# One state-space piece between the halves of the compression weights, keys and values turned two units earlier

## What is computed

```
xn = rms_norm(x, mix_norm_g)
a_q, a_kv, a_g, l_x, l_g, s_z, s_xbc, s_dt, m_g = [xn @ w for w in split(w_in)]
y_a = nsa_branch(a_q, a_kv, a_g, ...)     # attention: compressed, selected, window
y_b = rglru_branch(l_x, l_g, ...)         # causal conv, gates, recurrence
y_c = ssd_branch(s_z, s_xbc, s_dt, ...)   # causal conv of s_xbc, state-space mixer
x = x + merge(y_a, y_b, y_c, m_g) @ w_out
x = x + peer_ffn(rms_norm(x), ...)

# in nsa_branch, for keys and for values (n_cmp = 15 blocks of 32 positions):
blk = t[:, cmp_idx] + pe
compress = gelu(blk @ w1) @ w2            # w1 is 2048 x 256
k_cmp = rms_norm(compress(k_c, ...)); v_cmp = compress(v_c, ...)
```

## Time and profile before

| | us |
|---|---|
| median of three runs (2522.91 to 2526.2) | 2523.36 |
| the profiled execution | 2521.18 |
| its span | 2519.3 |

### The profile page before, as it was taken

The page is one execution under the profiler, slowest core; times in us unless marked ns, Lnnn a source line. Parts: engine busy times, 40 slices in busy tenths (PEclk is TensorE's granted clock), DMA queues, the critical chain, the costliest instruction groups (busy, mean ns, idle before and its releaser), DMA issues.

```text
span 2519.3 us, 43785 instructions
## 1 busy us (share of the span) xinstructions
PE 2464.8 (98%) x18006; PEld 2290.4 (91%) x18006; DVE 1591.2 (63%) x2554; ACT 1314.9 (52%) x1934; POOL 797.9 (32%) x436
## 2 busy tenths in 40 slices
PE   8899999999999999999998999999999999999999
PEld 8898999999999998888898989999999999888887
DVE  6878676498244555555677886764973455555555
ACT  5486663444554444444554965644445444444443
POOL 0011200288888830000000112003888888200000
PEclk9999999999999999999999999999999999999999
DMA  6533345355444445566555333453554444555554
GB/s 254 187 134 118 101 143 184 133 185 180 168 141 142 143 168 194 193 213 233 184 184 184 120 127 107 148 178 134 185 184 161 141 143 143 176 192 193 194 194 171
DMA packets 95956, 419.26 MB, mean 166 GB/s; under 512 B 10768, under 2 KB 11152, under 8 KB 78864
## 3 DMA queue, kind: packets, MB, share of 16 engines
q1 hardware_dynamic: 95760, 416.47, 48.0%
HBM read 415.38 MB, written 1.05 MB: 165 GB/s over the span
## 4 chain that ended last, share of the span: by engine, by line
PE 91%; DVE 4%; DMA 3%; ACT 2%; POOL 0%; issue 0%; SPq 0%; DVEq 0%
PE bank L2034 26%; PE bank L365 18%; PE bank L367 18%; PE bank L366 18%; PE bank L2015 5%; DMA xr<-in_xstream 1%; PE bank L761 1%; PE bank L738 1%; PE bank L722 1%; DVE ring_lo L356 1%; DMA ring<-in_wstream 1%; PE bank L1878 1%; PE bank L778 1%; PE bank L857 1%; PE bank L870 1%; POOL xr_lo L1736 0%
## 5 line engine op out<-in xcount | busy, mean ns | idle before, releaser
L1731 ACT ACTIVATE xr_hi<-xr 128x1024 fp32r<-128x1024 f32 x512 | 542.6, 1060 | 782.4 <-DMA xr<-in_xstream 782.1
L1736 POOL TENSOR_TENSOR xr_lo<-xr,xr_hi 128x1024 fp32r<-128x1024 f32 x256 | 620.7, 2428 | 428.3 <-ACT xr_hi L1731 427.8
L365 PE MATMUL bank<-featH,xr_hi 128*128 128x256 f32 x2048 | 586.7, 286 | 2.6 <-POOL xr_lo L1736 2.6
L366 PE MATMUL bank<-featL,xr_hi 128*128 128x256 f32 x2048 | 575.6, 281 | 0.0
L367 PE MATMUL bank<-featH,xr_lo 128*128 128x256 f32 x2048 | 575.5, 281 | 0.0
L1736 DVE TENSOR_TENSOR xr_lo<-xr,xr_hi 128x1024 fp32r<-128x1024 f32 x256 | 313.6, 1225 | 303.2 <-ACT xr_hi L1731 302.9
L365 PEld LDWEIGHTS bank<-featH,xr_hi 128*128 128x128 f32 x2048 | 386.2, 189 | 3.3 <-issue 1.8
L366 PEld LDWEIGHTS bank<-featL,xr_hi 128*128 128x128 f32 x2048 | 386.2, 189 | 0.0
L367 PEld LDWEIGHTS bank<-featH,xr_lo 128*128 128x128 f32 x2048 | 386.1, 189 | 0.0
L365 PE MATMUL bank<-featH,ring_hi 128*128 128x256 f32 x1232 | 354.5, 288 | 17.4 <-DVE ring_lo L356 16.2
L366 PE MATMUL bank<-featL,ring_hi 128*128 128x256 f32 x1232 | 348.8, 283 | 0.0
(11 more groups left out here) (347 smaller groups left out, 3986.0 us busy)
## 6 DMA issues: line engine op xcount, KB each, us to landing
xr<-in_xstream SPq DMA_DIRECT2D x512, 512.0 KB, 3.3
ring<-in_wstream SPq DMA_DIRECT2D x128, 1024.0 KB, 4.9
smw<-in_small SPq DMA_DIRECT2D x4, 617.0 KB, 9.1
first<-in_wstream SPq DMA_DIRECT2D x4, 512.0 KB, 7.0
first<-in_wstream SPq DMA_DIRECT2D x2, 1024.0 KB, 8.2
subk<-in_subkeys SPq DMA_DIRECT2D x2, 1024.0 KB, 7.0
x<-in_x SPq DMA_DIRECT2D x2, 512.0 KB, 6.0
big<-in_mix_row SPq DMA_DIRECT2D x2, 512.0 KB, 5.0
```

The costliest lines, as they stand in the source:

```text
L365: PE.matmul(o, s_hi_lo[0], m_hi_lo[0], start=first, stop=False)
L366: PE.matmul(o, s_hi_lo[0], m_hi_lo[1], start=False, stop=False)
L1731: A.activation(xr_hi[:, m % XR], xr[:, m % XR], ACT.Copy).then_inc(s_xhi, 1)
L1736: (PO if m < NKEY else V).tensor_tensor(xr_lo[:, m % XR], xr[:, m % XR], xr_hi[:, m % XR].bitcast(F32), ALU.subtract).then_inc(s_xlo_pool ...
```

## The change

Pieces 14, 15 and 16 change places in the stream: the first state-space piece becomes piece 14 (`FIRST_XBC`) and stands between the halves of the compression weights, which are now 12, 13 and 15, 16. The keys and values are turned ahead of piece 10, not behind it. TensorE's new order is: 9, `kv_turned`, 10, 11, first half, 14, second half, two groups of queries, 17, small transposes and two groups of queries, 18, second compression layer, 19, transpose of the compressed keys, scores. ScalarE makes the high part of 14 between the copies of 10 and 11, and that of 17 ahead of the copy of 14; VectorE makes the low part of 14 ahead of the second rotation and that of 17 after the first convolution step. `kcmpT` now comes after `filler(19)`.

```diff
-UNSPLIT = range(2 * W1K, 2 * XBC0)
+W1_HALVES = ((2 * W1K, 2 * W1K + 1), (2 * W1K + 3, 2 * W1K + 4))
+FIRST_XBC = 2 * W1K + 2
+UNSPLIT = W1_HALVES[0] + W1_HALVES[1]
+SPLIT = tuple(u for u in range(PIECES) if u not in UNSPLIT)
...
-                        for u in range(FIRST, LX + 3):
+                        for u in range(FIRST, LX + 2):
                             unit(u)
...
                         for t in range(NT):
                             kv_turned(t)
+                        unit(LX + 2)
                         unit(LX + 3)
...
+                        hidden(0)
+                        unit(FIRST_XBC)
+                        hidden(1)
                         for n in range(2):
                             q_turned(n)
-                        unit(XBC)
+                        unit(XBC + 1)
...
                         for n in range(2, 4):
                             q_turned(n)
-                        unit(XBC + 1)
+                        unit(XBC + 2)
...
                         mm.then_inc(s_co, 1)
-                        unit(XBC + 2)
+                        unit(XBC + 3)
                         pe.wait_ge(s_ckn, past(s_ckn) + 1)
                         PE.transpose(bank[7][:, 0:NCMP], ck[:], ident[0:NCMP, 0:NCMP]).then_inc(s_ckt, 1)
-                        unit(XBC + 3)
...
-                        for n in range(3):
+                        for n in range(2):
                             take(LX + n, lxT[:, 2 * n:2 * n + 2, PAD:])
...
+                        take(LX + 2, lxT[:, 4:6, PAD:])
+                        split_hi(act, FIRST_XBC)
                         take(LX + 3, lxT[:, 6:8, PAD:])
                         A.activation(gsig[:], tok_kv[:, :, GATE:GATE + 48], ACT.Sigmoid).then_inc(s_sig, 1)
-                        for n in range(HIS):
-                            split_hi(act, XBC + n)
-                        act.wait_ge(s_proj, past(s_proj) + UNSPLIT.stop)
+                        split_hi(act, XBC + 1)
+                        take(FIRST_XBC, xbcT[:, 0:2, PAD:])
+                        act.wait_ge(s_proj, past(s_proj) + UNSPLIT[3] + 1)
...
-                        filler(XBC)
+                        for n in range(2, 4):
+                            split_hi(act, XBC + n)
+                        filler(XBC + 1)
...
-                        filler(XBC + 1)
+                        filler(XBC + 2)
...
-                        filler(XBC + 2)
+                        filler(XBC + 3)
                         act.wait_ge(s_ckt, past(s_ckt) + 1)
                         A.activation(kcmpT[:], bank[7][:, 0:NCMP], ACT.Copy).then_inc(s_cktev, 1)
-                        filler(XBC + 3)
...
+                        split_lo(dve, FIRST_XBC)
                         q_rope(1)
...
                         for k in range(CONV):
                             lru_conv(k, 0)
-                            if k == 1:
-                                split_lo(dve, XBC)
+                            if k == 0:
+                                split_lo(dve, XBC + 1)
                         q_taken(0)
                         q_taken(1)
                         lru_conv(0, 1)
+                        split_lo(dve, XBC + 2)
                         lru_conv(1, 1)
-                        split_lo(dve, XBC + 1)
                         q_taken(2)
                         q_taken(3)
                         lru_conv(2, 1)
-                        split_lo(dve, XBC + 2)
+                        split_lo(dve, XBC + 3)
                         lru_conv(3, 1)
...
-                        split_lo(dve, XBC + 3)
...
+        stream[l, 2 * W1K + 2:2 * XBC0 + 1] = stream[l, [2 * XBC0, 2 * W1K + 2, 2 * W1K + 3]]
```

More of the change, by code:

```diff
@@ L299, in nth @@
             def nth(u):
-                return u if u < UNSPLIT.start else u - len(UNSPLIT)
+                return SPLIT.index(u)
             def piece(n):
-                return n if n < UNSPLIT.start else n + len(UNSPLIT)
+                return SPLIT[n] if n < len(SPLIT) else PIECES
             def load(sp, u):
@@ L525, in place @@
                     def place(u):
-                        if u < UNSPLIT.start:
+                        if u < UNSPLIT[0]:
                             return u
+                        if u == FIRST_XBC:
+                            return UNSPLIT[0]
                         if u < XBC + 5:
@@ L653, in mixer_tensor, with hidden @@
                             kv_turned(t)
+                        unit(LX + 2)
                         unit(LX + 3)
-                        for half in range(2):
+                        def hidden(half):
                             w1 = []
-                            for j in range(2):
-                                u = UNSPLIT.start + 2 * half + j
+                            for j, u in enumerate(W1_HALVES[half]):
                                 pe.wait_ge(s_blk, past(s_blk) + 2 * half + j + 1)
@@ L954, in filler @@
                             if u < LG:
-                                dst = xbcT[:, 2 * (u - XBC):2 * (u - XBC) + 2, PAD:]
+                                f = 0 if u == FIRST_XBC else 2 * (u - XBC)
+                                dst = xbcT[:, f:f + 2, PAD:]
                             elif u < MG:
```

## The result

| | before | after |
|---|---|---|
| median, us | 2524.43 (9 runs, 2520.99 to 2527.8) | 2531.16 (9 runs, 2528.94 to 2533.05) |
| the profiled execution | 2521.18 | 2531.91 |
| its span | 2519.3 | 2530.0 |
| its mean granted clock | 0.996 | 0.992 |

A forecast was written before the change was run, and what follows sets the result against it. TensorE, busy 98% of the span, was taken as the bound; gaps of 8.1 us a layer would become 7.15, gaining 0.95 a layer, 1.9 in two: 2521.5 us against the median 2523.36, range 2516.5 to 2526.5.

The forecast's parts named there:

- Keys and values earlier, the first half at 82.65: Layer 0, first compression half: follows piece 11 directly at 82.65, so the 0.54 us stall goes.
- Piece 14 at 86.4, to end at 92.25: Layer 0, between the compression halves: piece 14 runs 86.4 to 92.25, and the second half's 0.85 us stall goes.
- Second load 7.8 after its request, a gap of 1.7: Piece 17's load, second of two: ScalarE begins on it 7.8 us after the request; gap 1.7 where 3.83 stood.
- Piece 18 at 108.65 behind a gap of 2.85, VectorE in the way: Ahead of piece 18: six VectorE steps put its low part 10.05 us after the previous one, leaving a 2.85 gap.
- Scores behind a gap of 2.5, put down to `kcmpT`: Compressed scores: wait 2.5 us for ScalarE's `kcmpT`, behind piece 19's copy and 22's high part; start at about 124.5.
- I take 'kept' for all three.: TensorE's clock assumed to stay at full rate behind the new gaps of 1.7, 2.85 and 2.5 us.
- and 1.5 for each that is not: Price in us of each new gap behind which TensorE's clock is not kept.
- Behind the scores the order is unchanged … so the gain stays: After the scores: VectorE and ScalarE wait for TensorE again, so 0.95 us a layer, 1.9 in two, stays gained.
- The slower one: Rival: the clock falls at all three gaps, 4.5 us a layer, 2530.5; chance 0.06.
- The first rival: Clock falls at the 2.85 gap: 1.5 a layer, 2524.5, or 2523.0 in one layer; chance 0.27 for one or both.
- The credit for before: Before's piece 16, 7.36 us against 5.85 at full clock: 1.5 counted among the 8.1 lost per layer.
- The profiled execution: Before's profiled run, 2521.18, lay 2.2 below the median 2523.36; its forecast 2519.3 became 2521.5 against that median.

The follow-up runs named there:

- e3: Changed kernel with VectorE's list alone reordered, low parts of 18, 19 and 20 ahead of steps not yet awaited: 2518.99 us, ratio 0.9984 to before.
- e2: Changed kernel with ScalarE's copy `kcmpT` ahead of its copy of piece 19 and the high part of 22: 2522.54 us, ratio 0.9989 to before.
- e5: Kernel before with 28 filling matmuls on TensorE in its 3.83 stall ahead of piece 16, the wait kept: 2525.2 us, ratio 1.0005 to before.
- e7: Kernel before with VectorE's copies of two query groups and low part of 17 right behind the low part of 16: 2522.62 us, ratio 0.9996.
- e6: Kernel before with only the keys and values turned ahead of piece 10: 2524.23 us, ratio 1.0000 to before.
- e9: e4 with 18 filling matmuls at the 2.41 stall, ahead of the second query tile's first projection: 2511.6 us, ratio 0.9953 to before.
- e8: e4 with 18 filling matmuls meant for the 2.41 stall but one projection early, where TensorE had no stall: 2517.47 us, ratio 0.9976 to before.
- e1: Changed kernel with filling matmuls on TensorE, 22 ahead of piece 18 and 18 ahead of the scores, waits kept: 2523.75 us, ratio 1.0000 to before.
- e4: Changed kernel with the edits of both e2 and e3: 2511.25 us, ratio 0.9956 to before.
- e10: e4 run again, unchanged, on another chip, for comparison with e9: 2511.56 us, ratio 0.9953 to before.

## Why the prediction was wrong, step by step

*Keys and values earlier, the first half at 82.65.* Held: 82.90, no stall.

*Piece 14 at 86.4, to end at 92.25.* Held: 86.67 and 92.52.

*Second load 7.8 after its request, a gap of 1.7.* Nearly: ScalarE began on it at 93.91, 7.4 after the end of the first half (82.90 + 3.65), and the gap was 1.18 (1.28 in layer 1), 0.3 below what I had named as right. The estimate from the Trainium skill ("DMA: Bandwidth & Descriptors", Anatomy of one DMA), 6.8, missed by a little more on the other side (0.6 against 0.4).

*Piece 18 at 108.65 behind a gap of 2.85, VectorE in the way.* Held: 108.42, 2.87, the low parts 10.06 apart. e3, which takes VectorE out of the way, shows the cause: the stall goes to nothing.

*Scores behind a gap of 2.5, put down to `kcmpT`.* The gap held (2.44), and e2 shows its cause: with the copy moved, 0.32 is left. The start, 125.65, missed the forecast's bound of 125 by the 1.4 that piece 18 took longer.

*"I take 'kept' for all three."* This is the step that failed. The clock was kept at 1.18 and fell at 2.87 and at 2.44, in both layers. The choice rested on two rows of one execution, 2.41 kept and 3.36 fallen, read as if a length between them decided. The same 2.41 is followed by a fall in both layers of after, and in e5 one and the same stall of 2.87 did both. What I had to take from the earlier trace rows was that a stall of 2.4 had been kept once, not that it is safe; a bound from both sides would have put one or both falls into the likeliest case. The better reading stood beside it, that the same gap may cost nothing in one place and half-rate matmuls in another: in e5 the same stall has 1.00 in layer 0 and 0.50 in layer 1. I had worked it out from the Trainium skill ("TensorE: Matmul & The Clock Gate", Part 1), which says that the monitor's windows run freely, whatever the kernel does; e5 agrees with it, and no run shows the windows themselves.

The sizes fit: a gain of 1.9 was forecast and a loss of 6.7 measured, 8.6 apart. The two falls cost 1.4 and 2.9 in layer 0, 8.7 in two layers.

*"and 1.5 for each that is not".* Right for the fall in front of piece 18 (7.28 against 5.85), half of what the fall in front of the scores cost: 1.6 in the scores and 1.3 in piece 20, 2.9 together. The low stretch there lasted 6.8 us and not 3.4. When I expected e2 I put that down to the 32 small matmuls of the scores. The runs don't bear it out: low stretches of 6.8 us also stand in front of dense matmuls only (e2 in layer 1, e5 in layer 1, e7 in both), and in layer 1 of e3 the one behind the scores' stall is 3.4. All low stretches of this place, in all profiles, are 3.4 or 6.8 us long; what decides between the two stays open.

*"Behind the scores the order is unchanged … so the gain stays".* True of the order, not of the clock: the fall runs on into piece 20, and the stall at 235 had one too. That third fall comes without the change as well: the profile of before lacks it in both layers, but e5, e6 and e7 have it in five of six.

*The rivals.* The slower one gave 2530.5 and the time was 2531.16, but not by its mechanism: it wanted the clock to fall at all three gaps, and at 1.18 it was kept. Two falls at its price give 3.0 a layer and 2527.5; the dearer second fall makes it 4.4 a layer and 2530.2, and the median of before moved up by 1.1 with six more runs. It got a chance of 0.06 since I tied it to the shortest gap; a fall at 2.87 and 2.44 with 1.18 kept, the likeliest of the mixed cases, stood nowhere. The first rival (a fall at 2.85 alone, 2524.5) was half of the truth.

*The credit for before.* The sum by gaps counts 1.5 for before's slow piece 16 and lets 1.5 more stall stand behind the new 17. e5 shows that this balance was right: at full clock before is as long as it was.

*The profiled execution.* I noted that it lay 2.2 below the median and took it for an offset. It had fewer falls than most, neither of the two at the stalls of 2.41. The runs of before differ in their mean clock, 0.993 to 0.996, and their times go with it in the rough (medians of 2524.5 at 0.993, 2524.9 at 0.994 and 2522.2 at 0.995). A sum made on a run with few falls has too few of them in both kernels.

## What to carry to other kernels

Where TensorE is busy for 98%, a stall has two prices, its length and the half-rate matmuls behind it, and the second made the difference here: the stalls of the place add up to 6.5 us a layer before and after (0.54 + 0.85 + 3.83 + 1.35 against 1.18 + 2.87 + 2.44), and the kernel lost 0.26% because two of the new ones cost clock on the path. Here the clock fell behind many stalls of 2.24 us and more, not behind each, and once behind one of 1.53. So take a stall of 2 us as one that may lower it unless many executions say otherwise, and count the half-rate matmuls behind it with the longer of the low stretches seen. When a piece is moved on one engine, go through the lists of the others for steps that nobody awaits yet: here two convolution steps on VectorE and the order of one small copy on ScalarE turned the loss into 0.45% of gain.

## What the runs showed of the hardware

- The length of a stall doesn't decide alone. 2.87 us was followed by 1.2 GHz in one layer of e5 and by 2.4 GHz in the other, 2.56 by a fall in e9 and 2.60 by none in e8; 2.41 was kept in before and not in after. Stalls of 1.69 (e9) and 2.15 (e1) were kept. The shortest with a fall just behind them are 2.24 in e6 and 1.53 in e6, the latter 1.3 us of matmuls behind one of 1.28.
- A fall can come where TensorE hardly stood. Ahead of the compressed scores of e2, e4, e8, e9 and e10 lay 0.32 us, and in four of these ten layers the clock fell during or just behind them (0.72 over 124 to 128 in e2, 0.64 over 120 to 124 in e10). In e4, the same kernel as e10, the stretch has 1.00.
- Low stretches were 3.4 or 6.8 us long, both in front of dense matmuls and in front of the scores. They cost 1.4 (after, piece 18) and 2.9 (after, scores and piece 20).
- Not settled: what makes the same stall fall in one run and not in another, and what makes a low stretch the longer one. The profiled executions show stretches, the others only their mean clock.
